# Modulation chunks of the first two slabs' columns on TensorE instead of VectorE, with the condition loaded first

## The reference, cut to what matters

```python
cond = jax.nn.silu(c)
for l in range(DEPTH):
    mod = cond @ w_mod[l] + b_mod[l]                 # 2048 -> 6 * 2048
    sh1, sc1, g1, sh2, sc2, g2 = jnp.split(mod[:, None, :], 6, axis=-1)
    u = x * (1.0 + sc1) + sh1
    proj = u @ w_in[l]                               # 2048 -> 6144
    # q, k, v: rotary and dilated attention; B, C, h: gated short convolution
    mixed = _group_rms_norm(jnp.concatenate([attn, conv], axis=-1), mix_norm_g[l])
    x = _layer_norm(DEEPNORM_ALPHA * x + (1.0 + g1) * (mixed @ w_out[l]), ln1_g[l], ln1_b[l])
    u = x * (1.0 + sc2) + sh2
    ff = jnp.square(jax.nn.relu(u @ w_ff1[l])) @ w_ff2[l]
    x = _layer_norm(DEEPNORM_ALPHA * x + (1.0 + g2) * ff, ln2_g[l], ln2_b[l])
```

## Time and profile before

| what | value |
|---|---|
| median of three runs | 2389.97 us |
| profiled execution, its own time | 2390.11 us |
| its span in the profile | 2388.4 us |
| PE busy | 2270.1 us, 95% |
| DVE busy | 1728.5 us, 72% |
| ACT busy | 1115.9 us, 47% |
| bytes moved | 623.14 MB |

### The profile page before, as it was taken

The page is one execution under the profiler, slowest core; times in us unless marked ns, Lnnn a source line. Parts: engine busy times, 40 slices in busy tenths (PEclk is TensorE's granted clock), DMA queues, the critical chain, the costliest instruction groups (busy, mean ns, idle before and its releaser), DMA issues.

```text
span 2388.4 us, 30251 instructions
## 1 busy us (share of the span) xinstructions
PE 2270.1 (95%) x10384; PEld 1881.5 (79%) x10384; DVE 1728.5 (72%) x1913; ACT 1115.9 (47%) x1424; POOL 227.3 (10%) x400
## 2 busy tenths in 40 slices
PE   3689999989999999999998999999999999999997
PEld 2577888778888888888877888887888888888885
DVE  6898888868777767667878877877766555555566
ACT  2235543356435435435454554435643543543543
POOL 2211111110101101000010100101000000000000
PEclk9789999989999999999999999999999999999998
DMA  9987988958888888887965777886677666666563
GB/s 354 390 289 283 306 324 316 325 211 283 285 283 293 287 276 298 276 276 268 321 242 184 267 262 257 287 293 220 224 237 242 206 213 215 213 205 193 177 228 123
DMA packets 174733, 623.14 MB, mean 261 GB/s; under 512 B 19728, under 2 KB 20496, under 8 KB 174096
## 3 DMA queue, kind: packets, MB, share of 16 engines
q1 hardware_dynamic: 114128, 407.50, 49.8%
q0 software_dynamic: 55296, 201.35, 24.8%
q10 hardware_dynamic: 5184, 12.59, 1.6%
HBM read 619.27 MB, written 2.10 MB: 260 GB/s over the span
## 4 chain that ended last, share of the span: by engine, by line
PE 84%; DVE 8%; DMA 3%; issue 3%; ACT 2%; ACTq 0%; SPq 0%; DVEq 0%; POOLq 0%
PE bank L1249 25%; PE bank L1251 25%; PE bank L1250 25%; DVE mod_acc L770 3%; PE bank L1350 2%; PE bank L1325 2%; DVE w_lo L755 1%; DMA raw<-w_out_dram 1%; DMA Z<-w_mod_dram 1%; ACT w_hi L455 1%; PE bank L1263 1%; PE bank L1264 1%; PE bank L1265 1%; ACT utmp L496 0%; DVE xt L877 0%
## 5 line engine op out<-in xcount | busy, mean ns | idle before, releaser
L755 DVE TENSOR_TENSOR w_lo<-raw,w_hi 128x1024 fp32r<-128x1024 f32 x768 | 937.8, 1224 | 563.7 <-ACT w_hi L455 561.7
L455 ACT ACTIVATE w_hi<-raw 128x1024 fp32r<-128x1024 f32 x768 | 812.4, 1059 | 1129.2 <-PE bank L1251 988.4
L1249 PE MATMUL bank<-w_hi,u_hi 128*128 128x512 f32 x1744 | 695.3, 399 | 0.3 <-DVE u_lo L813 0.3
L1251 PE MATMUL bank<-w_lo,u_hi 128*128 128x512 f32 x1744 | 682.0, 391 | 0.0
L1250 PE MATMUL bank<-w_hi,u_lo 128*128 128x512 f32 x1744 | 681.5, 391 | 0.0
L1249 PE MATMUL bank<-w_hi,m_hi 128*128 128x512 f32 x1216 | 476.9, 392 | 2.8 <-DVE m_lo L813 2.6
L1251 PE MATMUL bank<-w_lo,m_hi 128*128 128x512 f32 x1216 | 474.5, 390 | 0.0
L1250 PE MATMUL bank<-w_hi,m_lo 128*128 128x512 f32 x1216 | 474.3, 390 | 0.0
L770 DVE SCALAR_TENSOR_TENSOR mod_acc<-mod_raw,cond,mod_acc 128x1024 f32<-128x1024 f32 x300 | 383.7, 1279 | 0.6 <-DMA mod_raw<-w_mod_dram 0.6
L1251 PEld LDWEIGHTS bank<-w_lo,u_hi 128*128 128x128 f32 x1744 | 328.9, 189 | 70.0
L1249 PEld LDWEIGHTS bank<-w_hi,u_hi 128*128 128x128 f32 x1744 | 329.5, 189 | 68.6 <-issue 1.4
(11 more groups left out here) (128 smaller groups left out, 1116.5 us busy)
## 6 DMA issues: line engine op xcount, KB each, us to landing
raw<-w_ff_dram SPq DMA_DIRECT2D x512, 512.0 KB, 4.2
mod_raw<-w_mod_dram POOLq DMA_DIRECT2D x320, 512.0 KB, 5.4
raw<-w_in_dram SPq DMA_DIRECT2D x192, 512.0 KB, 5.2
Z<-w_mod_dram POOLq DMA_DIRECT2D x64, 512.0 KB, 9.1
raw<-w_out_dram SPq DMA_DIRECT2D x64, 512.0 KB, 5.7
gate<-b_rows_dram ACTq DMA_DIRECT2D x4, 1024.0 KB, 4.9
Z<-ln_g_dram ACTq DMA_DIRECT2D x16, 256.0 KB, 6.3
Z<-ln_b_dram ACTq DMA_DIRECT2D x16, 256.0 KB, 7.0
```

The costliest lines, as they stand in the source:

```text
L455: nc.scalar.activation(w_hi[:, j % AHEAD, :], raw[:, j % RAW, :], ACT.Copy).then_inc(hi_ready, 1)
L755: nc.vector.tensor_tensor(w_lo[:, j % AHEAD, :], raw[:, j % RAW, :], w_hi[:, j % AHEAD, :].bitcast(F32), ALU.subtract).then_inc(lo_ready, 1)
L1249: nc.tensor.matmul(o, hi[:, k, tok], wh, start=(k == 0), stop=False)
L1251: ins = nc.tensor.matmul(o, hi[:, k, tok], wl, start=False, stop=(k == KC - 1))
```

## The change

- SP loads the condition first (`c_in`), then the identity and the `b_mod` columns (`first_in`), then the first block of x. The six other constants follow; only the rotary step and ACT's negated sine wait for them.
- All 64 chunks of the head are taken from DVE. PE multiplies each with eight matmuls: a 128x128 block of the chunk is stationary and the column of `cond` is moving (`start_chunk`). The results are eight columns of `tb[1]`, and accumulate there over the 16 chunks of a quarter. A ninth small matmul closes the quarter and carries the semaphore `sum_done`.
- The partition sum of the head falls away, since the matmuls sum over partitions themselves. Both turns of a quarter use `tb[0]`; `tb[1]` is the sums' own bank during the head. The head's turns and sums are no jobs any more.
- The 16 chunks of quarter 0 stand at the front of PE's program. The 16 of quarter q+1 stand in fours behind groups i = 0 to 3 of quarter q.
- A new semaphore `chunk_used` (one step a chunk, from PE) frees the slots of `start_raw`, and SP's first weight load waits for eight chunks of it. `mod_used` counts only the later chunks, so its targets are lowered by 64 (`START_SHARE` = 0).

```diff
@@ SyncE
-            small = [(idn[:], ident), (cs[:], cos), (sn[:], sin), (msk[:], mask), (mod_b[:], b_mod),
-                     (mixg[:], mix_g), (cw[:], conv_w), (cc_in[:], cond_c), (lnc[:], ln_cols)]
-            for dst, src in small:
-                sp.dma_start(dst, src).then_inc(small_in, 16)
+            sp.dma_start(cc_in[:], cond_c).then_inc(c_in, 16)
+            sp.dma_start(idn[:], ident).then_inc(first_in, 16)
+            sp.dma_start(mod_b[:], b_mod).then_inc(first_in, 16)
...
             load_x(0)
-
-            sp.wait_ge(mod_used, 4)
+            small = [(cs[:], cos), (sn[:], sin), (msk[:], mask), (mixg[:], mix_g), (cw[:], conv_w), (lnc[:], ln_cols)]
+            for dst, src in small:
+                sp.dma_start(dst, src).then_inc(small_in, 16)
+
+            sp.wait_ge(chunk_used, 8)
@@ GpSimd, the refill of start_raw
-                    pool.wait_ge(mod_used, 8 * r + (k - 7))
+                    pool.wait_ge(chunk_used, 8 * r + (k - 7))
@@ ScalarE, start_job
-                job = JOB[("start turn", i)]
-                split(i, i % 2, job, job % 2, u_hi, 2 * i,
-                      lambda c: (u_scale[:, c:c + 1], u_shift[:, c:c + 1]))
-                split_high(job // 2 + 1, i % 2, job % 2, u_hi, 2 * i)
+                act.wait_ge(turn_done, i + 1)
+                if i >= 2:
+                    act.wait_ge(split_ready, i - 1)
+                for c in range(2):
+                    k = 2 * i + c
+                    ins = nc.scalar.activation(utmp[:, i % 2, c * SEQ:(c + 1) * SEQ], tb[0][:, c * SEQ:(c + 1) * SEQ],
+                                               ACT.Identity, bias=u_shift[:, k:k + 1], scale=u_scale[:, k:k + 1])
+                ins.then_inc(turn_read, 1)
+                act.wait_ge(turn_read, i + 1)
+                nc.scalar.activation(u_hi[:, 2 * i:2 * i + 2, :], utmp[:, i % 2, :], ACT.Copy).then_inc(split_hi, 1)
@@ VectorE, start_scale and start_quarter
-                job = JOB[("start", q)]
-                reduced(q, job)
-                dve.wait_ge(t_read[job % 2], job // 2 + 1)
+                dve.wait_ge(sum_done, q + 1)
+                cols = slice(q * SC, (q + 1) * SC)
+                nc.vector.tensor_tensor(mod_col[:, cols], tb[1][:, 0:SC], mod_b[:, cols], ALU.add).then_inc(sum_read, 1)
+                dve.wait_ge(sum_read, q + 1)
...
-                    if q + 1 < START_SLABS:
-                        start_mods(q + 1, k, 1)
-                    else:
-                        mod_next(k)
+                    if q + 1 == START_SLABS:
+                        mod_next(2 * i)
+                        mod_next(2 * i + 1)
@@ VectorE, mixer
-                                if i < 4:
-                                    start_mods(q + 1, 4 + 3 * i, 3)
@@ TensorE
+            def start_chunk(n, k):
+
+                q = n * KC + k
+                if n == 0 and k == 0:
+                    pe.wait_ge(cond_ready, 1)
+                if n and k == 0:
+
+                    pe.wait_ge(sum_read, n)
+                pe.wait_ge(start_in[q % 8], 16 * (q // 8 + 1))
+                for c in range(SC):
+                    ins = nc.tensor.matmul(tb[1][:, c:c + 1], start_raw[:, q % 8, c * P:(c + 1) * P], cond[:, k:k + 1],
+                                           start=(k == 0 and c == 0), stop=(k == KC - 1 and c == SC - 1))
+                ins.then_inc(chunk_used, 1)
+                if k == KC - 1:
+                    nc.tensor.matmul(tb[1][:, SC:SC + 1], idn[:], ones[:, 0:1], start=True, stop=True).then_inc(sum_done, 1)
...
             def start_fill(q):
 
                 pe.wait_ge(x_in[q], 16)
-                for i in range(2):
-                    c0 = 4 * q + 2 * i
-                    turn(JOB[("start turn", 2 * q + i)], lambda c, t: xt[:, t, (c0 + c) * P:(c0 + c + 1) * P])
-                    if i == 0:
-                        reduce_slab(q % 2, JOB[("start", q)], KC * (q + 1))
+                start_turn(2 * q)
+                start_turn(2 * q + 1)
 
             def start_units(side):
 
+                for k in range(KC):
+                    start_chunk(0, k)
                 start_fill(0)
...
+                    if q + 1 < START_SLABS and i < START_LABELS - 2:
+                        for k in range(4 * i, 4 * i + 4):
+                            start_chunk(q + 1, k)
                     if q + 1 < START_SLABS and i == START_LABELS - 2:
                         start_fill(q + 1)
```

More of the change, by code:

```diff
@@ L142 @@
 START_UNITS = 3
+START_SHARE = 0
 START_LABELS = GK * START_UNITS
@@ L163, in transpose_jobs @@
         modded = layer < DEPTH - 1
[L164 to L168, removed]
-        else:
+        if layer:
             add(("fill", 2 * layer), 8)
@@ L272, in build @@
         sbank, obank = banks[6], banks[7]
+        c_in = sem("c_in")
+        first_in = sem("first_in")
         small_in = sem("small_in")
+        chunk_used = sem("chunk_used")
+        sum_done = sem("sum_done")
+        sum_read = sem("sum_read")
+        turn_done = sem("turn_done")
+        turn_read = sem("turn_read")
         x_in = [sem(f"x_in{q}") for q in range(START_SLABS)]
@@ L433, in _ @@
                     for k in range(MODS):
-                        pool.wait_ge(mod_used, MODS * r + (first + k - MODS + 1))
+                        pool.wait_ge(mod_used, MODS * r + (START_SHARE + k - MODS + 1))
                         pool.dma_start(mod_raw[:, k:k + 1, :], chunk(r * MODS + (first + k))).then_inc(mod_in[k], 16)
@@ L725, in mlp @@
                         relu_square(base + w)
-            act.wait_ge(small_in, 16 * 9)
+            act.wait_ge(c_in, 16)
             act.wait_ge(ones_ready, 3)
             nc.scalar.activation(cc_e[:], cc_in[:], ACT.Exp, scale=-1.0).then_inc(cond_exp, 1)
+            prepare(0, 0, first=True)
+            prepare(0, 1, first=True)
+            start_fill(0)
+            prepare(0, 2, first=True)
+            prepare(0, 3, first=True)
+            act.wait_ge(small_in, 16 * 6)
             nc.scalar.activation(nsn[:], sn[:], ACT.Copy, scale=-1.0).then_inc(cond_exp, 1)
-            for j in range(AHEAD):
-                prepare(0, j, first=True)
-            start_fill(0)
             for layer in range(DEPTH):
@@ L774, in mod_next @@
             def mod_next(q):
-                first = START_SLABS * KC
+                first = START_SHARE
                 mod_step(None, q % KC, q // KC % 2, mod_raw[:, q % MODS, :], mod_in[q % MODS],
@@ L953, in start_quarter, with some @@
             def start_quarter(q):
-                def one(k):
-                    if q + 1 < START_SLABS:
-                        start_mods(q + 1, k, 1)
-                    else:
-                        mod_next(k)
-                one(0)
+                def some(i):
+                    if q + 1 == START_SLABS:
+                        mod_next(2 * i)
+                        mod_next(2 * i + 1)
                 start_scale(q)
-                one(1)
+                some(0)
                 start_low(2 * q)
-                one(2)
+                some(1)
                 start_low(2 * q + 1)
-                one(3)
             def residual(unit, par, s, alpha):
@@ L1069, in rotate @@
                     dve.wait_ge(pair_used, 8 * base + p + 1)
+                    if layer == 0 and u == 0:
+                        dve.wait_ge(small_in, 16 * 6)
+                        dve.wait_ge(cond_exp, 2)
                     start = layer == 0 and u < START_UNITS
@@ L1351, in turn, with start_turn @@
                 ins.then_inc(t_done, 1)
+            def start_chunk(n, k):
[11 more added lines that the diff above has]
+                    nc.tensor.matmul(tb[1][:, SC:SC + 1], idn[:], ones[:, 0:1], start=True, stop=True).then_inc(sum_done, 1)
+            def start_turn(i):
+                if i:
+                    pe.wait_ge(turn_read, i)
+                for c in range(2):
+                    for t in range(T):
+                        ins = nc.tensor.transpose(tb[0][:, c * SEQ + t * P:c * SEQ + (t + 1) * P],
+                                                  xt[:, t, (2 * i + c) * P:(2 * i + c + 1) * P], idn[:])
+                ins.then_inc(turn_done, 1)
             def start_fill(q):
                 pe.wait_ge(x_in[q], 16)
[L1356 to L1360 removed]
+                start_turn(2 * q)
+                start_turn(2 * q + 1)
             def start_units(side):
+                for k in range(KC):
+                    start_chunk(0, k)
                 start_fill(0)
```

18 lines of the change are left out of this document (8 added, 10 removed).

## The result

| | before | after |
|---|---|---|
| median | 2390.91 us (4 runs, 2387.24 to 2394.49) | 2535.23 us (4 runs, 2532.61 to 2537.71) |
| profiled execution, its span | 2390.11, 2388.4 us | 2535.98, 2534.3 us |
| turn of q behind group 22 | 159.83 us | 305.13 us |
| from there to the end of the span | 2228.6 us | 2229.2 us |

The changed kernel is 6.0% slower (ratio 1.0604, interval 1.0587 to 1.0622). The two lower rows of the table say where: all of it lies ahead of the marker.

The account below looks back on a forecast made before the run. PE, busy 95% of the span, was taken as the bound, so head changes reach the end: marker 64.3 + 72.4 + 150.4 + 17.4 = 304.5, 144.7 later; 2390.1 + 144.7 = 2534.8, said 2535 us; own range 2515 to 2560, full range 2470 to 2590.

Parts of the forecast that it names:

- Nothing is given back or lost behind the marker: From the turn of q behind group 22 to the end: 2228 us as before, change under 5 us.
- The start at 6.5: PE's first chunk matmul, after cond, identity, b_mod and chunk 0: near 6.5 us; 16.5 if the load order helped nothing.
- Quarter 0, 16 x 3.4 = 54.4: Quarter 0's 16 chunks on PE: 3.4 us each at half clock, from 6.5 to 60.9 us.
- The first group at 64.3: First wide group: closing matmul 0.4 and 3.0 us as before after quarter 0's chunks, so 64.3 us.
- The blocks, 11.0, and the groups between, 4.6: Head behind quarter 0's chunks: four chunks 11.0 us, a group starting at half clock 4.6, together 15.6.
- The clock: PE in the head: narrow matmuls count as idleness; clock rises after 4.1 us of wide work, falls 3.2 us after it.
- Rivals A and B: Head clock: full on narrow matmuls, 2442 or 2465 us, 16%; or half all through, 2580 us, 14%.
- A's milder form: Head: narrow matmuls only keep a clock wide ones released; marker 235, 2465 us; full-clock rival as a whole 16%.
- The step between quarters, 5.0: Behind group i = 4: PE waits for a weight split, bias and scale, ACT and the turn, 5.0 us with handovers.
- The marker at 304.5, 144.7 later: Turn of q behind group 22: 64.3 + 72.4 + 150.4 + 17.4 = 304.5 us, against 159.8 before.
- Rival C: Head: chunk loads hide under wide matmuls or waits, so faster; at 0.8 us a chunk marker 140, 2370 us; chance 3%.
- DVE's chunks as what paces the head before: Kernel before, head: DVE's chunks pace the quarters; groups resume at 77.63, 31 us after the first.

Follow-up runs that it names:

- The order late again: Changed kernel with the condition back in its old place among the constants (eighth of nine), all 64 chunks still on TensorE: 2546.98 us.

## Why the prediction was right, point by point

- **Nothing is given back or lost behind the marker.** Right: 2228.6 and 2229.2 us. The release of VectorE after the head bought nothing.
- **The start at 6.5.** 5.95. PE waited for `b_mod`, which landed 4.1 us after its issue, not 6.8. The order late again gave 18.1, not 16.5.
- **Quarter 0, 16 x 3.4 = 54.4.** 54.6 at the pitch of half clock. The price of a chunk, taken from the eight partition-sum matmuls, was right to 1%, and halving the matmuls shows that it goes with them.
- **The first group at 64.3.** 64.64, by two misses that cancel. The start was 0.5 us early, and from the closing matmul to the first group it took 4.1 us (60.55 to 64.64) where 3.4 were put: both turns stand behind the sum now, and the prediction had taken the distance of the kernel before, with one.
- **The blocks, 11.0, and the groups between, 4.6.** Over the head the blocks are 10.9 and the groups 4.8 on average. In the first quarter: blocks 10.6 and 11.6 to the next wide matmul, groups 5.1, 4.2, 4.8 and 5.3. A pair took 14.8 (69.78 to 84.53), 16.4 and 16.2, on average 15.8 against 15.6.
- **The clock.** The mechanism was the uncertain step, weighed at 67% against 16% and 14%. That the lost clock is the price is now shown by experiment and not only read: with 64 moving columns the blocks kept full clock and the kernel was 73 us faster. Rivals A and B fell for the kernel as it is; the prices given to A's milder form (235, 2465) match the kernel in which that form was made true (235.35, 2462). The two times taken from the rows, a rise after 4.1 us and a fall after 3.2 us, were middles of a wide spread: by pitch and PEclk the rise came 2.9 to 5.6 us after the start of the first five groups that began at half clock, and the fall 2.1 to 3.8 us after the groups that stand ahead of the first five blocks. The chance that B was given had its reason: the group at 111.78 took 5.3 us, at half clock to its end.
- **The step between quarters, 5.0.** From 132.18, the end of group 4, to the next wide matmul at 136.62: 4.4 us, 3.43 of it idle, and 4.8 us in the two later quarters, with ScalarE's and VectorE's splits ahead of `utmp` as worked out.
- **The marker at 304.5, 144.7 later.** 305.13, 145.3 later. The sum held at 0.6 us, and that closeness is luck, since larger misses cancelled. The two wide groups on end behind a step took 5.6 and 6.5 us, not 7.4, as the clock was up already or rose soon; the groups between blocks took about 0.2 us more each than put; and the last stretch took 18.9 us (286.27 to 305.13), not 17.4, since its first 5 us ran at half clock. The prediction's own range of 2515 to 2560 is the fair measure of what it knew.
- **Rival C, loads that hide.** They did not hide. From start to start a chunk at full clock cost 1.70 us alone behind a group and 1.77 in blocks with 64 columns; break-even was put at 1.1. So the 1.9 read from the earlier trace rows was a tenth too high. Turning the operands gave 1.76 by its row.
- **DVE's chunks as what paces the head before.** Right: behind quarter 0 VectorE waited 0.2 us for chunks, and TensorE 25.3 us for VectorE's sums. What went unasked is how near the next bound stood. Nothing in the forecast hung on it, but the expectation of 8 to 11 us for the load order alone did, and it brought 3.8.
- **One sign to look for was wrong.** PEclk was to read 0.50 in quarter 0, and it read 1.00, as no change of clock had been recorded yet. The pitch showed half clock.

By the Trainium skill's rule for a load ("TensorE: Matmul & The Clock Gate", LDWEIGHTS: columns over 1.2 in ns, 107 ns, with no clock named) the time was estimated at 2457 us. The pitch in quarter 0, 213 ns, decides against it here; at full clock it agrees, with 106 ns (1.70 us for 16 records).

## What to carry to other kernels

A matrix times a vector on TensorE, with the matrix stationary, costs a load for every 128x128 block; price it by a row of the same shape and dtype, at both clocks, and ask whether the stretch around it keeps the clock. Moving work off an engine that looks like the bound pays only until the next bound, and here it came soon: a few chunks in TensorE's idle places gave 0.4%, all of them cost 6%. Transfers that run at their full rate need not be the bound; look at whether the engine that uses them waits. An early start is worth what it is ahead of: about 12 us where TensorE was the bound throughout, 3.8 where the transfers bounded the first quarter.

## What the runs showed of the hardware that was not expected

- 54.8 us of float32 matmuls with 64 moving columns, without a break, ran at the pitch of half clock (0.214 us a record), while blocks of the same matmuls behind wide ones stayed at full clock (0.11 us a record).
- With one moving column the record's pitch is the same as with 64 at half clock, 0.213 us: there 64 columns cost nothing over one. At full clock it is 0.106 us with one and 0.11 us with 64.
- Two queues at once shared the transfers evenly, in the kernel with the condition first: the chunks came 2.56 us apart (26.82, 29.38) and the weights beside them too (ScalarE's splits at 24.94 and 27.50), twice the 1.28 us that 512 KB take at 410 GB/s.
